# Expert loop of a Hymba-style layer on one core: the slot-number copies move behind the first GpSimd subtraction, and the last block's down products move to PSUM banks 0 and 1

## The reference, cut to what matters

```python
for e in range(MOE_EXPERTS):
    he = jax.nn.silu(t @ w_gate[e]) * (t @ w_up[e])
    y = y + gates[:, e:e + 1] * (he @ w_down[e])
```

## Time and profile before

| | us |
|---|---|
| median of 3 runs (1296.68, 1296.98, 1304.98) | 1296.98 |
| the profiled execution's own time | 1294.63 |
| its span | 1292.8 |
| outside the span | 1.8 |
| PE busy | 1127.9 (87%) |
| DVE busy | 844.1 (65%) |
| ACT busy | 626.1 (48%) |
| POOL busy | 397.8 (31%) |

### The profile page before, as it was taken

One profiled execution on the slowest core, in us unless ns is written; L12 is line 12 of the kernel. 1 busy time (PEld: TensorE's weight loads), 2 busy tenths in 40 slices (PEclk: granted clock), 3 DMA queues, 4 the chain that ended last, 5 costly groups with the idle time before them and its releaser, 6 DMA issues.

```text
span 1292.8 us, 21444 instructions
## 1 busy us (share of the span) xinstructions
PE 1127.9 (87%) x7030; PEld 897.4 (69%) x7030; DVE 844.1 (65%) x1211; ACT 626.1 (48%) x979; POOL 397.8 (31%) x292
## 2 busy tenths in 40 slices
PE   4899999999969689999999369898989998989885
PEld 4898899999967365555555258676767776767763
DVE  4697656444394464544442778878777787878877
ACT  5432111276423353433432237766766675767663
POOL 1121111122001001111111125555545565666650
PEclk9999999999978899999999679999999899999998
DMA  6116222222154400011114935786998958657343
GB/s 244 61 60 84 65 73 76 82 68 83 25 111 182 183 1 1 34 49 49 50 66 143 360 103 173 263 294 189 339 354 273 321 151 296 202 195 211 86 152 152
DMA packets 85156, 190.73 MB, mean 148 GB/s; under 512 B 7744, under 2 KB 27712, under 8 KB 84432
## 3 DMA queue, kind: packets, MB, share of 16 engines
q1 hardware_dynamic: 78464, 165.69, 37.6%
q0 software_dynamic: 6624, 24.12, 8.0%
HBM read 220.61 MB, written 31.51 MB: 195 GB/s over the span
## 4 chain that ended last, share of the span: by engine, by line
PE 48%; DMA 14%; DVE 12%; issue 9%; ACT 7%; POOL 7%; SPq 1%; POOLq 1%; ACTq 0%; DVEq 0%
PE ps L452 13%; DMA h_d<-par,sml 13%; PE ps L1740 9%; PE ps L2149 8%; POOL split L2103 5%; PE ps L1713 3%; PE ps L1690 2%; ACT split L2191 2%; PE ps L1373 1%; PE ps L1347 1%; PE ps L1707 1%; PE ps L1727 1%; PE ps L527 1%; ACT mem L1633 1%; PE ps L1714 1%
## 5 line engine op out<-in xcount | busy, mean ns | idle before, releaser
L2149 PE MATMUL ps<-split 128*128 128x512 f32 x1728 | 433.9, 408 | 55.9 <-POOL split L2103 43.3
L2149 PEld LDWEIGHTS ps<-split 128*128 128x128 f32 x1728 | 331.1, 196 | 141.2 <-POOL split L2103 57.6
L2191 ACT CAST split<-weights 128x1024 fp32r (+1 forms) x288 | 298.6, 1051 | 157.9 <-PE ps L2149 142.7
L2243 DVE TENSOR_TENSOR split<-weights,split 128x1024 fp32r<-128x1024 f32 x216 | 312.6, 1494 | 87.8 <-ACT split L2191 85.3
L452 PE MATMUL ps<-xsplit,wsplit 128*128 128x384 f32 (+2 forms) x1584 | 277.2, 331 | 6.8 <-DVE xsplit L406 6.8
L452 PEld LDWEIGHTS ps<-xsplit,wsplit 128*128 128x128 f32 x1584 | 253.6, 192 | 13.3 <-DVE xsplit L406 7.7
L2103 POOL TENSOR_TENSOR split<-weights,split 128x1024 fp32r<-128x1024 f32 x72 | 174.4, 2422 | 137.0 <-ACT split L2191 136.7
L238 POOL TENSOR_TENSOR wsplit<-mem,wsplit 128x1024 fp32r<-128x1024 f32 x22 | 54.5, 2477 | 263.1 <-ACT wsplit L307 263.1
L1740 PE MATMUL ps<-mem 128*128 128x512 f32 x256 | 118.2, 606 | 0.7 <-DVE mem L1578 0.7
L1550 DVE TENSOR_REDUCE sml<-ps 128x1 f32<-128x1040 f32 (+7 forms) x64 | 46.6, 769 | 81.1 <-PE ps L1690 81.1
L1633 ACT COPY mem<-ps 128x512 f32<-128x512 f32 (+3 forms) x48 | 21.4, 481 | 132.0 <-PE ps L1707 86.3
(11 more groups left out here) (411 smaller groups left out, 1352.4 us busy)
## 6 DMA issues: line engine op xcount, KB each, us to landing
weights<-in_w_down SPq DMA_DIRECT2D x26, 2048.0 KB, 16.3
weights<-in_w_gate SPq DMA_DIRECT2D x50, 1024.0 KB
weights<-in_w_up SPq DMA_DIRECT2D x50, 1024.0 KB
mem<-in_w_in SPq DMA_DIRECT2D x22, 512.0 KB, 4.0
mem<-in_x SPq DMA_DIRECT2D x10, 512.0 KB, 4.1
mem<-in_w_out SPq DMA_DIRECT2D x1, 4096.0 KB, 12.9
h_d<-mem SPq DMA_DIRECT2D x8, 512.0 KB, 3.0
xn_d<-mem SPq DMA_DIRECT2D x8, 512.0 KB, 2.6
```

What stands on the lines that cost most here:

```text
L2149: mm = nc.tensor.matmul(ps[:, bank + h, :], x, w[place % RING][:, 512 * h:512 * h + 512], start=(k == 0 and p_ == 0), stop=(k == n - 1 and ...
L2191: nc.scalar.copy(WH[place % RING], raw(kind, k, q)).then_inc(wh_ready, 1)
L2243: nc.vector.tensor_tensor(WL[place % RING], raw(kind, k, q), WH[place % RING].bitcast(F32), ALU.subtract).then_inc(wl_dve, 1)
```

## The change

On POOL, `columns` moves from the round's head to behind the low part of place 3, with its wait on ye_stored; `gather` is now the head. In round 23 there is no scatter ahead, so `columns` stays at the head there, without the slot numbers and without the wait. In round 23 the down products go to PSUM banks 0 and 1 in place of 4 and 5, PE no longer waits for the outputs of block 22 before them, and DVE makes HLO ahead of `split_outputs_of`. The final stage uses the bank pairs 2, 6, 4 in place of 0, 2, 6, and waits for the outputs of block 22 before its first product.

```diff
--- before.py
+++ after.py
@@ -2090,10 +2090,11 @@
                 pool.sem_inc(ix_seen, 1)
                 pool.indirect_dma_start(XG[:, par], None, xn_d, bass.IndirectOffsetOnAxis(ap=ixc[:, par:par + 1], axis=0)).then_inc(xg_loaded[par], 16)
 
-            def columns(b, par):
+            def columns(b, par, stays):
                 pool.wait_ge(slots_ready, 2)
                 pool.sem_inc(ix_seen, 1)
-                nc.gpsimd.tensor_copy(sixc[:, par:par + 1], SIX[:, bass.ds(b, 1)])
+                if not stays:
+                    nc.gpsimd.tensor_copy(sixc[:, par:par + 1], SIX[:, bass.ds(b, 1)])
                 nc.gpsimd.tensor_copy(tokc[:, par:par + 1], TOKF[:, bass.ds(b, 1)])
                 nc.gpsimd.tensor_copy(wcol[:, par:par + 1], WS[:, bass.ds(b, 1)]).then_inc(wcol_ready, 1)
 
@@ -2112,15 +2113,18 @@
             def body(j, par, first, last):
                 b = 2 * j + par
                 q, q_next = buffers(pool, b, par, last)
-                if not first:
-                    pool.wait_ge(ye_stored, 16 * b - 16)
-                columns(b, par)
+                if par and last:
+                    columns(b, par, True)
                 if has(par, last, 2):
                     pool.wait_ge(xgt_ready, 2 * b + 2)
                     gather(b + 2, par)
                 for place, (kind, k) in enumerate(chunks(not has(par, last, 1))):
                     if place % RING == RING - 1:
                         lower(b, place, kind, k, q_next if kind == "gu" else q)
+                    if place == RING - 1 and not (par and last):
+                        if not first:
+                            pool.wait_ge(ye_stored, 16 * b - 16)
+                        columns(b, par, False)
                     if place == 2 * RING - 1 and (par or not first):
                         pool.wait_ge(ye_copied, 2 * b)
                         pool.sem_inc(ix_seen, 1)
@@ -2174,11 +2178,11 @@
                 pe.wait_ge(hl_ready, b + 1)
                 if has(par, last, 2):
                     turn_x(j + 1, par)
-                if par or not first:
+                if (par or not first) and not (par and last):
                     pe.wait_ge(ye_copied, 2 * b)
                 for place, (kind, k) in enumerate(chunks(not has(par, last, 1))):
                     if kind == "down":
-                        product(b, place, k, FF // P, HH[:, k], HLO[:, k], 4)
+                        product(b, place, k, FF // P, HH[:, k], HLO[:, k], 0 if par and last else 4)
 
             return blocks(pe, body)
 
@@ -2235,7 +2239,7 @@
             nc.scalar.activation(SD2[:, 0:1], con[:, C_ONES:C_ONES + 1], ACT.Sqrt).then_inc(sd2_ready, 1)
             act.wait_ge(chunk_used, down_used(2 * pairs - 1, True))
             for h in range(2):
-                nc.scalar.activation(XH[:, 1, 4 * h:4 * h + 4].rearrange("p k q -> p (k q)"), ps[:, 4 + h, :], ACT.Identity,
+                nc.scalar.activation(XH[:, 1, 4 * h:4 * h + 4].rearrange("p k q -> p (k q)"), ps[:, h, :], ACT.Identity,
                                      scale=wcol[:, 1:2]).then_inc(sg_ready, 1)
 
         def dve_weights_lower(dve, b, place, kind, k, q):
@@ -2269,7 +2273,7 @@
                 return v[:, par, 4 * h:4 * h + 4].rearrange("p k q -> p (k q)")
 
             def output_lower(par, h):
-                nc.vector.scalar_tensor_tensor(flat(XL, par, h), ps[:, 4 + h, :], wcol[:, par:par + 1], flat(XH, par, h).bitcast(F32),
+                nc.vector.scalar_tensor_tensor(flat(XL, par, h), ps[:, h if par else 4 + h, :], wcol[:, par:par + 1], flat(XH, par, h).bitcast(F32),
                                                ALU.mult, ALU.subtract).then_inc(ye_copied, 1)
 
             def split_outputs_of(b, par):
@@ -2302,12 +2306,12 @@
                     if place % RING < RING - 1:
                         lower(b, place, kind, k, q_next if kind == "gu" else q)
                     if place == RING - 1:
-                        if par and last:
-                            split_outputs_of(b - 1, 0)
-                        elif par or not first:
+                        if (par or not first) and not (par and last):
                             outputs_of(b - 1, 1 - par, first)
                         dve.wait_ge(hh_ready, b + 1)
                         nc.vector.tensor_tensor(HLO, ps[:, 6, :].rearrange("p (k q) -> p k q", k=4), HH.bitcast(F32), ALU.subtract).then_inc(hl_ready, 1)
+                        if par and last:
+                            split_outputs_of(b - 1, 0)
                 if has(par, last, 1):
                     hidden(b + 1, 1 - par)
                 if has(par, last, 2):
@@ -2327,7 +2331,7 @@
 
         def bank(t):
 
-            return (0, 2, 6)[t % 3]
+            return (2, 6, 4)[t % 3]
 
         def sp_final(sp, pairs):
             sp.wait_ge(ye_stored, 32 * pairs - 32)
@@ -2349,6 +2353,7 @@
                 return mm
 
             pe.wait_ge(slot_rows_ready, 2)
+            pe.wait_ge(ye_copied, 4 * pairs - 2)
             for t in range(3):
                 terms(t, 0)
             pe.wait_ge(ye_copied, 4 * pairs)
```

## The result

The changed kernel takes 1251.29 us (median of 4 runs, 1245.67 to 1252.38); the kernel before takes 1296.83 us in the same comparison (4 runs, 1295.42 to 1304.98). The ratio is 0.9628, with a 95% interval of 0.9578 to 0.9677: 45.5 us less, against 42.6 predicted (1254 was forecast for the median). The profiled execution took 1252.38 us with a span of 1250.6.

What follows compares the result with a forecast made beforehand. A loop through the scatter's landing and POOL's queue was taken to bound the kernel. 9.8 + 27.2 + 7.6 - 3.5 + 1.5 = 42.6 us off 1294.63 gave 1252.0 profiled, 1254 median; range 1242 to 1262.

Steps and rivals of the forecast that it cites:

- the new period: Expert rounds outside the weight stretch: 18.4 us each, bounds 17.9 and 18.9, saving 9.8 and 27.2 us.
- POOL's queue behind it: Head of a round: the scatter's landing plus 4.7 us of POOL's queued work ends last ahead of place 3.
- ran without the wait: Two rounds of the kernel before, 17.90 and 18.23 us long, said to lack the wait; basis for the period.
- The weights: Rounds 6 to 10: the weight loads' end, not POOL, sets the time; together 7.6 us saved.
- the term for loads that start earlier: Rounds 6 to 10: loads start earlier as the rounds do; 2.5 us gained, bounds 0 and 5.
- The late scatter: DVE's outputs ahead of place 4: landings later than 10.6 us cost PE; 3.5 us lost, bounds 0 to 9.
- The end: Final stage: HLO moves ahead, but the last load's landing limits the gain to 1.5 us, bounds 0 and 3.
- ACT's waits for in_w_up: Sign in the new profile: ACT's waits for up weights grow from a few us to over 10.
- DVE's waits ahead of the outputs: Sign in the new profile: DVE's waits before making the outputs grow; no size given.
- DVE did not take the wait over: Rival: in shorter rounds late scatter landings hold DVE in most rounds; 1262 or 1270 us, chance 0.12.
- The weights hold rounds 6 to 10 and no others: Rival: weight loads also hold other rounds, losing half their gain, 18.5 us; 1273 us, chance 0.08.
- does not hold the scatter up: Rival, slower: the earlier gather delays the scatter's landing to 14.6 us; 1334 us, chance 0.04.

Runs made afterwards that it cites:

- e2: The changed kernel with POOL's part taken back, so only the end of the change remains: 1297.06 us, ratio 0.998 to the kernel before.
- e1: The kernel before with only POOL's part of the change, the end of the stage as before: 1254.26 us, ratio 0.9633.
- e3: The changed kernel with the wait for the scatter put back at the round's head, the copies staying behind place 3: 1268.39 us, ratio 0.9746.
- e5: The kernel before with no weights loaded after the first two experts (outputs wrong): 1286.55 us, one run.
- e6: The changed kernel with no weights loaded after the first two experts (outputs wrong): 1246.74 us, one run.
- e7: The changed kernel with SP issuing gate and up loads first and the down load one round later: 1241.96 us, ratio 0.9523 to the kernel before.
- e4: The changed kernel with only the slot numbers copied behind place 3, the other two copies right behind the gather: 1251.63 us, ratio 0.962.
- e8: e7 with the final stage's residual load cut in two halves, the gain row between them: 1239.42 us, ratio 0.9509 to the kernel before.

## Why the prediction was right

**The cause and its size.** The chain and PE's wait for place 3 pointed at the right place, and the new period, forecast at 18.4 us, was measured at 18.38 (rounds 11 to 21) and 18.30 (rounds 3 to 5). It was right because it came from two rounds of before in which PE ran through, not from adding up the parts. Rounds 3 to 5 and 11 to 21 gave 10.1 and 27.4 us, for 9.8 and 27.2. That the stretches agree to 0.3 us is luck: the other pair of executions of the same two loops, e2 and e1, gives 6.9 and 36.1 us. For rounds 3 to 21 together the forecast was 9.8 + 27.2 + 7.6 - 3.5 = 41.1 us; the pairs give 43.7 and 50.0.

**What the step lumped together.** It said that the landing ends last ahead of place 3, "plus 4.7 us of POOL's queue behind it". e3 and e5 show that these are two causes. In ordinary rounds the landing (7.3 us) alone would have cost nothing; the copies ahead of the gather did. In rounds with an 11 us landing the wait cost as well. In the profiles of rounds 11 to 21 they share about evenly, 14.7 and 12.7 us; by the medians the copies weigh more. The forecast did not need the split, because the change moves both.

The trace of before already had the hint. The prediction says that two of its rounds "ran without the wait", but in the one of 18.23 us only PE did. POOL waited:

```profile
1151.05 0.18 POOL L2096 COPY sml<-sml 128x1 int32 x1 [0.85 <-DMA h_d<-par,sml]
```

Its three copies were over by 1151.46, since they took 0.17 to 0.18 us each, and PE began the round at 1152.79. In round 21 the landing came at 1211.12, only 0.72 us ahead of PE, and the copies lasted until 1213.85.

**The weights.** Rounds 6 to 10 gave 6.2 us for 7.6 in the profile of the change, and 9.2 in e1, whose loop is the same. The mechanism was right: taking the loads away (e6) or issuing them in another order (e7) frees these rounds by 8.5 and 10.5 us, by 5.4 and 7.4 against the 98.4 us of e1 and e4. Whether the term for loads that start earlier (2.5 us) was too large or too small can't be told: 6.2 lies below the sum of 7.6, and 9.2 above. What the forecast missed is why: the loads were held by SP's order, not only by bandwidth.

**The late scatter.** Priced at 3.5 us, cost next to nothing. The mechanism exists, as round 3 of e7 shows, but too few landings were late. After the change only one scatter of the 22 landed later than the 10.6 us that the prediction names, 11.1 us after its start (853.81), and PE then stood still 0.21 us ahead of place 4:

```profile
857.01 6.18 PE L2153 MATMUL ps<-split 128*128 128x512 f32 x24 [0.21 <-DVE split L2247]
```

From 984 to 1186 us PE never waited for DVE, and rounds 11 to 21 are no shorter when no scatter is late (203.05 in e6 for 202.21). One reading behind this term was wrong. The low part of place 4 was put at 1.2 us, ready at 1216.8; in that round of before it took 3.61 us, beside POOL's low part. In the same round after the change it took 1.53 us, since POOL's low part of place 3 was nearly over. (A smaller slip: the scatter that `columns` waits for is 1216.0 - 1203.73 = 12.3 us old by then, not 10, which only helps the step.)

**The end.** 1.5 us forecast, and 67.44 - 65.92 = 1.5 measured, by the named limit: DVE idled 4.18 us for the load. e8 took that limit away, and then PE's products were next.

**The sum.** In the spans the terms are 10.1 + 6.2 + 27.4 + 1.5 = 45.2 us; rounds 0 to 2 are 0.1 longer, and the part before the experts, which the change does not touch, was 2.9 us longer in this execution. That gives 42.2 = 1292.8 - 1250.6. A loss of 3.5 us that did not come and a gain of 1.4 us too much nearly cancel with the extra 2.9 us, so the forecast for the profiled execution, 1252.0 against 1252.38, is closer than its steps were, by luck. The 2.35 us that I carried over from profile to median went the other way: here the median lies 1.1 below the profiled run.

**The signs that did not come.** ACT's waits for in_w_up were to grow to over 10 us; they went from 7.4 to 8.6. DVE's waits ahead of the outputs were to grow; they fell from 3.8 to 2.7 us. The copies were long in most rounds, as said, but not in all: in 17 of the 22 rounds.

**The rivals.** DVE did not take the wait over (2.7 us against POOL's 65). The weights hold rounds 6 to 10 and no others, as e6 shows. The gather, now issued while the scatter is in flight, does not hold the scatter up: the scatter's median landing is 7.3 us as before. What I had not priced is the other direction, small as it is. The gather's own landing:

```profile
DMA to landing us min/median/max: 4.3/7.2/9.7
```

It was 4.3/6.3/9.0 us before. In round 21 PE turns the rows 12.7 us after the gather's start (1184.68 - 1171.96), so this is hidden.

## What to carry to other kernels

A long wait in the profile is not what its removal is worth: POOL waited 64 us in e3 and 65 us before, with 31 us between the kernels. Ask what stands in the queue behind the waiting instruction and how long each piece really takes beside its neighbours; moving cheap work out from between a wait and what is urgent can bring half of the gain or more. And look in the same trace for iterations that already ran without the stall: their period was the better forecast here. And compare two executions of the same kernel stage by stage before a difference in one stage is called a finding. In a queue of loads, let the one that is wanted first go first, even if a buffer for the other comes free earlier.

## What the runs showed of the hardware

- A GpSimd copy of 128 single elements took 0.17 to 0.18 us, or, beside DVE's low parts, 1.17 to 1.20 us (in 17 rounds of 22 after the change); one that began in the middle of a low part took 0.46 (1211.12, before). DVE's low parts were no longer beside the copies (two in 2.35 us with and without them). Beside POOL's 2.4 us low part one of them took 3.61 us, and three took 5.88 (before, from 1215.64).
- After an idle stretch of 4.83 us, 24 matmuls took 7.18 us before, 7.33 in e5 and 8.36 in e1. After 2.16 us they took 5.72 to 5.75 in after, e2, e3, e4 and e6, but 7.33 in e7 and 7.32 in e8. The granted clock was 1.00 in after from 1211.55 to 1217.25 us (the level of 2.4 GHz), 0.79 in e8 from 1204 to 1212 us and 0.66 in e1 from 1216 to 1225 us, both between the levels of 1.2 and 2.4 GHz in the mean. So the idle time just ahead does not settle the clock, and why e7 and e8 got less is open.
- The indirect scatter lands in 6.8 to 7.5 us without weight loads (e5) and in up to 11.4 us with the weight loads beside it (before).
